# A hybrid two-block transformer on one core: every second chunk of the mixers' first products in halves, with its low half made by an accumulating transfer

## The reference

```python
h = rmsnorm(x, norm_mix[l])
(u_ssm, q_lat, kv_lat, k_rope, hg_q, hg_f, hg_i, hg_g, gate_logits) = jnp.split(h @ w_in[l], split_at, axis=-1)
y_ssm = s5_mixer(u_ssm, ...)
y_mla = mla_mixer(q_lat, kv_lat, k_rope, ...)
y_hg = hgrn2_mixer(hg_q, hg_f, hg_i, hg_g, ...)
gates = jax.nn.sigmoid(gate_logits)
x = x + (gates[0] * y_ssm + gates[1] * y_mla + gates[2] * y_hg) @ w_out[l]
x = x + memory_cross_attention(rmsnorm(x, norm_cross[l]), ...)
x = x + swiglu_ffn(rmsnorm(x, norm_ffn[l]), ...)
```

## Time and profile before

| | us |
|---|---|
| median of 3 runs | 1920.4 (1919.24 to 1921.8) |
| the profiled execution | 1917.89 |
| its span, first to last instruction | 1916.1 |
| PE busy | 1804.5 (94%) |
| DVE busy | 1232.3 (64%) |
| ACT busy | 867.0 (45%) |
| POOL busy | 277.2 (14%) |
| mean granted TensorE clock | 0.979 of full speed |

### The profile page before, as it was taken

The page is one execution under the profiler, slowest core; times in us unless marked ns, Lnnn a source line. Parts: engine busy times, 40 slices in busy tenths (PEclk is TensorE's granted clock), DMA queues, the critical chain, the costliest instruction groups (busy, mean ns, idle before and its releaser), DMA issues.

```text
span 1916.1 us, 27084 instructions
## 1 busy us (share of the span) xinstructions
PE 1804.5 (94%) x10038; PEld 1446.3 (75%) x10038; DVE 1232.3 (64%) x1895; ACT 867.0 (45%) x1413; POOL 277.2 (14%) x274
## 2 busy tenths in 40 slices
PE   7999989989999999999888999998899999989998
PEld 6676667569998866677577998656799864779987
DVE  7996755445667893855455566565677645566775
ACT  4224444355444422444355445336555543555553
POOL 4015453020000003557012000100100000010000
PEclk9999999999999999999999999998999999799999
DMA  6444442436566444445054666431455644135554
GB/s 160 130 130 152 133 152 89 143 105 180 160 187 188 119 127 142 133 133 177 28 191 116 194 184 192 147 110 56 141 177 163 193 153 121 56 107 170 169 187 138
DMA packets 192359, 274.61 MB, mean 143 GB/s; under 512 B 25616, under 2 KB 129540, under 8 KB 192228
## 3 DMA queue, kind: packets, MB, share of 16 engines
q1 hardware_dynamic: 191364, 269.86, 46.2%
q0 software_dynamic: 864, 3.02, 0.6%
HBM read 271.78 MB, written 1.05 MB: 142 GB/s over the span
## 4 chain that ended last, share of the span: by engine, by line
PE 80%; DVE 7%; ACT 6%; issue 3%; SPq 1%; POOL 1%; DMA 1%; DVEq 0%; ACTq 0%; POOLq 0%
PE bank L400 46%; PE bank L398 23%; DVE WL L1165 2%; ACT WH L1452 2%; PE bank L671 1%; PE bank L585 1%; PE bank L593 1%; PE bank L1021 1%; PE bank L871 1%; PE bank L1041 1%; PE bank L488 1%; ACT HTH L1452 1%; DVE bank L2117 1%; POOL WL L1165 0%; PE bank L654 0%
## 5 line engine op out<-in xcount | busy, mean ns | idle before, releaser
L1165 DVE TENSOR_TENSOR WL<-W,WH 128x1024 fp32r<-128x1024 f32 x304 | 372.5, 1225 | 241.9 <-ACT WH L1452 233.0
L1452 ACT ACTIVATE WH<-W 128x1024 fp32r<-128x1024 f32 x328 | 347.5, 1059 | 302.3 <-PE bank L400 267.2
L400 PE MATMUL bank<-HTH,WH 128*128 128x256 f32 x1536 | 437.6, 285 | 19.6 <-DVE WL L1165 9.5
L400 PE MATMUL bank<-HTL,WH 128*128 128x256 f32 x1536 | 434.5, 283 | 0.0
L400 PE MATMUL bank<-HTH,WL 128*128 128x256 f32 x1536 | 434.5, 283 | 0.0
L400 PEld LDWEIGHTS bank<-HTH,WH 128*128 128x128 f32 x1536 | 294.5, 192 | 25.2 <-DVE WL L1165 11.8
L400 PEld LDWEIGHTS bank<-HTL,WH 128*128 128x128 f32 x1536 | 294.7, 192 | 0.1
L400 PEld LDWEIGHTS bank<-HTH,WL 128*128 128x128 f32 x1536 | 294.6, 192 | 0.0
L400 PE MATMUL bank<-WH,HTL 128*128 128x512 f32 x672 | 261.4, 406 | 0.0
L400 PE MATMUL bank<-WH,HTH 128*128 128x512 f32 x480 | 192.7, 402 | 18.5 <-POOL WL L1165 5.7
L400 PE MATMUL bank<-WL,HTH 128*128 128x512 f32 x480 | 188.5, 393 | 0.0
(11 more groups left out here) (405 smaller groups left out, 2495.8 us busy)
## 6 DMA issues: line engine op xcount, KB each, us to landing
W<-in_w_in SPq DMA_DIRECT2D x132, 512.0 KB, 3.7
W<-in_ffn_w_gate_up SPq DMA_DIRECT2D x176, 256.0 KB, 3.4
W<-in_w_up SPq DMA_DIRECT2D x176, 256.0 KB, 3.6
W<-in_ffn_w_down SPq DMA_DIRECT2D x44, 512.0 KB, 3.7
W<-in_w_down SPq DMA_DIRECT2D x44, 512.0 KB, 4.2
W<-in_w_out SPq DMA_DIRECT2D x32, 512.0 KB, 3.4
W<-in_ssm_w_glu SPq DMA_DIRECT2D x16, 512.0 KB, 4.3
W<-in_x_w_kv SPq DMA_DIRECT2D x16, 512.0 KB, 3.4
```

Source lines behind the costliest of these rows:

```text
L400: m = pe.matmul(out, at_a(a[x]), at_b(b[y]), start=(start and i == 0), stop=(stop and i == 2), skip_group_check=True)
L1165: eng.tensor_tensor(WL[:, m % HSLOTS, 0:width], W[:, n % RSLOTS, 0:width], h, ALU.subtract)\
L1452: copy = lambda dst, src, scale=1.0: act.activation(dst, src, ACT.Copy, scale=scale)
```

## The change

Of each of the six groups hf, hq, hi, hg, kv and ql the second and the fourth chunk are now products in halves, with the split kind "dma". There are 12 such chunks in a layer. ACT copies the high part (`WH`), and then writes the negative of the high part into `WL`. POOL waits for that (`negative`) and issues a transfer that reads the same chunk of the weights from memory again and adds it to `WL`; its landing completes the low part. The chunk's buffer in `W` is free once ACT has copied the high part. POOL now makes `mix_half` earlier: after `mix_scaled` and after PE has finished u3. Then it issues the twelve transfers, in order, and only after them come, in layer 0, the inverse frequencies and rope angles, and in both layers `lat_rstd`. The core of the diff:

```diff
+            if who == "dma":
+                return f"low_dma{m % HSLOTS}", 16 * sum(1 for _, w in splits[m % HSLOTS:m + 1:HSLOTS] if w == "dma")
...
-                chunk_release[n] = (s, v)
+                chunk_release[n] = ("high", high_done(m)) if low == "dma" else (s, v)
...
+                    src, slot, how = act, lambda k: k, low
+                    if halves and k0 // kstep % 2:
+                        src, slot, how = halves, half_slot, "dma"
+                        if k0 == kstep:
+                            pe.wait_ge(sem["mix_halves"], l + 1)
+                    n, w = chunk(tag, rows(wname, l, k0, kstep, c0, cols), kstep, cols, how)
...
-                    token_out((name, l), "w_in", l, HTF, KT, c0, 512, low=None)
+                    token_out((name, l), "w_in", l, HTF, KT, c0, 512, low=None, halves=mix_half, how="dma")
...
+            def add_chunk(m):
+                n, _ = splits[m]
+                _, (src,), k, cols = chunks[n]
+                pool.wait_ge(sem["negative"], negative_done(m))
+                dst = WL[:, m % HSLOTS, 0:k * cols].rearrange("p (k n) -> p k n", k=k)
+                pool.dma_start(dst, src, accum_op=ALU.add).then_inc(sem[low_done(m)[0]], 16)
...
+                pool.wait_ge(sem["mix_scaled"], l + 1)
+                wait_full(pool, ("u", l, 3))
+                signal(halves_of(mix_half, HTF, 2, 6), "mix_halves", l + 1)
+                split_to(split_before["ql", l, 1])
+                if l == 0:
...
-                signal(halves_of(mix_half, HTF, 2, 6), "mix_halves", l + 1)
...
                     signal(copy(WH[:, m % HSLOTS, 0:width], W[:, n % RSLOTS, 0:width]), "high", high_done(m))
+                    if who == "dma":
+                        signal(copy(WL[:, m % HSLOTS, 0:width], WH[:, m % HSLOTS, 0:width].bitcast(F32), -1.0),
+                               "negative", negative_done(m))
```

More of the change, by code:

```diff
@@ L320, in low_done, with negative_done @@
         def low_done(m):
-            who = "dve" if splits[m][1] == "dve" else "pool"
-            return f"low_{who}", sum(1 for _, w in splits[:m + 1] if (w == "dve") == (who == "dve"))
+            who = splits[m][1]
+            if who == "dma":
+                return f"low_dma{m % HSLOTS}", 16 * sum(1 for _, w in splits[m % HSLOTS:m + 1:HSLOTS] if w == "dma")
+            if who == "dve":
+                return "low_dve", sum(1 for _, w in splits[:m + 1] if w == "dve")
+            return "low_pool", sum(1 for _, w in splits[:m + 1] if w in ("pool", "both"))
         def high_done(m):
             return sum(1 for _, w in splits[:m + 1] if w != "both")
+        def negative_done(m):
+            return sum(1 for _, w in splits[:m + 1] if w == "dma")
         @block.tensor
@@ L406, in token_out, with token_steps @@
                     pass
-            def token_steps(tag, wname, l, act, K, c0, cols, low="dve", kstep=2, halves=None):
+            def token_steps(tag, wname, l, act, K, c0, cols, low="dve", kstep=2, halves=None, how="both"):
                 ps = [begin(*tag, tt) for tt in range(TT)]
@@ L413, in token_steps @@
                     if halves and k0 // kstep % 2:
-                        n, w = chunk(tag, rows(wname, l, k0, kstep, c0, cols), kstep, cols, "both")
+                        n, w = chunk(tag, rows(wname, l, k0, kstep, c0, cols), kstep, cols, how)
                         src, slot = halves, half_slot
@@ L521, in feature_out, with feature_steps @@
                     pass
-            def feature_steps(tag, wname, l, act, K, c0, tiles, low="dve", kstep=2, extra=0):
+            def feature_steps(tag, wname, l, act, K, c0, tiles, low="dve", kstep=2, extra=0, halves=None):
                 cols = tiles * P + extra
@@ L529, in feature_steps @@
                 for k0 in range(0, K, kstep):
-                    n, w = chunk(tag, rows(wname, l, k0, kstep, c0, cols), kstep, cols, low)
+                    src, slot, how = act, lambda k: k, low
[3 more added lines that the diff above has]
+                            pe.wait_ge(sem["mix_halves"], l + 1)
+                    n, w = chunk(tag, rows(wname, l, k0, kstep, c0, cols), kstep, cols, how)
                     need_rows(act, k0 + kstep)
@@ L534, in feature_steps @@
                         for k in range(kstep):
-                            m = product(ps[j // 2][:, (j % 2) * S:(j % 2) * S + S], w, act,
-                                        lambda a: a[:, k, j * P:j * P + P], lambda b: b[:, k0 + k, :],
+                            m = product(ps[j // 2][:, (j % 2) * S:(j % 2) * S + S], w, src,
+                                        lambda a: a[:, k, j * P:j * P + P], lambda b: b[:, slot(k0 + k), :],
                                         k0 + k == 0 and j % 2 == 0, k0 + k == K - 1)
@@ L542, in feature_steps @@
                             for k in range(kstep):
-                                m = product(kr[:, tt * extra:(tt + 1) * extra], act, w,
-                                            lambda a: a[:, k0 + k, tt * P:tt * P + P],
+                                m = product(kr[:, tt * extra:(tt + 1) * extra], src, w,
+                                            lambda a: a[:, slot(k0 + k), tt * P:tt * P + P],
                                             lambda b: b[:, k, tiles * P:cols],
@@ L702, in mixer_in @@
                 def mixer_in(name, c0, tiles, extra=0):
-                    return feature_steps((name, l), "w_in", l, HTF, KT, c0, tiles, low=None, extra=extra)
+                    return feature_steps((name, l), "w_in", l, HTF, KT, c0, tiles, low=None, extra=extra,
+                                         halves=mix_half)
                 def mixer_tokens(name, c0):
-                    token_out((name, l), "w_in", l, HTF, KT, c0, 512, low=None)
+                    token_out((name, l), "w_in", l, HTF, KT, c0, 512, low=None, halves=mix_half, how="dma")
                 def ssm_u(*qs):
@@ L801, in _ @@
                     ssm_out(l, 3)
-                pe.wait_ge(sem["mix_halves"], l + 1)
                 for n in range(2):
@@ L1344, in split_to @@
                         both_parts(m)
+                        lows[0] = m + 1
+                    elif splits[m][1] == "dma":
+                        add_chunk(m)
                         lows[0] = m + 1
```

## The result

The changed kernel takes 1975.6 us (median of 4 runs, 1974.1 to 1978.0), the kernel before 1919.8 in the same comparison (1917.2 to 1921.8): a ratio of 1.030 [1.0285, 1.0314], **3.0% slower**. The profiled execution took 1975.23 us, span 1972.4, clock 0.966; before 1917.89, 1916.1 and 0.979. By these two it is 57.3 us slower, where I had forecast 36.5.

What follows compares the result with a forecast made beforehand. PE was taken to bound the kernel. Layer 0's +20.3 us and layer 1's +16.2 made +36.5 on the profiled 1917.9, 1954.4; with 2.5 for the median of runs, 1957 us, range 1933 to 1981.

Steps and rivals of the forecast that it cites:

- the first add: Layer 1, hf's second chunk: PE waits for POOL's input halves (5.0 us) and an add of 6.5 us; +8.0 us.
- the other adds: Later halved chunks: supply takes 14.1 us against PE's 12.6, but bank stalls give most back; +1.5 us a layer.
- the clock: Lower granted clock after PE's idleness at the head: +3 us in layer 1, +1 in layer 0.
- the forecast's test: Sign of error: the forecast is wrong if PE's idle time in the two stages does not grow by some 40 us.
- PE's savings: Halved chunks of the six groups take PE less time: 6.4 us a layer, 12.9 in both.
- ACT's wait ahead of rb: Head of each layer: ACT must await and copy hf's second chunk before evicting rb; +15.1 us layer 0, +4.75 layer 1.
- evictions behind the splits: ACT does both splits of the next group before evicting, so PE waits for banks; +9.1 us layer 0, +5.4 layer 1.
- DVE's state-space chain is shifted by the same 15 and so stays ahead: Layer 0 head: DVE's chain moves about 15 us later, as PE does, so PE does not wait for it.
- The extra 11 MB of reads find the transfer engines half idle: The adds' second reads of weights have room on the transfer engines; SP's order is not delayed by them.
- POOL in layer 0: Frequencies and angles, 22.1 us, moved behind the twelfth add, stay hidden ahead of the latent sums with 3 us to spare.
- Slow adds as a rival: Each add takes 9.6 us, lengthening a pair of chunks to 7.8 us from 6.3; time 1980 us, chance 0.16.

Runs made afterwards that it cites:

- e5: Changed kernel with ACT's evictions of rb and of each group moved ahead of the splits and no adding transfers issued (low half incomplete): 1914.5 us, ratio 0.9978.
- e2: Changed kernel, but ACT evicts rb, BT, the parameters and the first bu group before the first splits, except one split in layer 0: 1954.1 us, ratio 1.0203.
- e4: On top of e2, ACT evicts hf, hq, hi, hg and kv after the next group's first split, before its second: 1945.4 us, ratio 1.0156.
- e1: Changed kernel without the 24 adding transfers, PE waiting for ACT's negative instead; ACT's copies and order kept, output wrong: 1956.7 us, ratio 1.0205.
- the small add: e4 with each adding transfer cut from 512 KB to a 64 KB corner, still issued and waited for: 1923.7 us, ratio 1.0035.
- e6: Changed kernel's six groups in halves, but POOL makes both halves itself, with no adding transfer and no ACT split ahead of rb: 1969.9 us, ratio 1.026.

## Why the prediction came out as it did

The direction, the place and the kind of each wait were right, and 1975.6 is inside the range, near its upper end. The forecast was 19 us short. By the changed kernel's own trace, term by term (the clock as weighed above; some of PE's work hides in the ends of the waits):

| term, both layers | predicted, us | in the trace, us |
|---|---|---|
| the head, up to hf | +19.9 | +19.9 (14.3, 5.6) |
| PE's shorter matmuls | -12.9 | -11.0 |
| the first add, with POOL's halves | +8.0 | +9.2 |
| the other adds | +3.0 | +14.3 |
| banks | +14.5 | +8.7 |
| lower clock from hf to uq | +4 | +12.7 |
| lower clock at uq in layer 0 | 0 | +3.4 |
| sum | +36.5 | +57.2 |

Two terms were far too small, then, the other adds and the clock, and one was too large, the banks. Outside these stretches the two executions differ by amounts that no run ties to the change: by the clock, 3.9 us more lost in the rest of layer 0 and 9.3 less from layer 1's uq on, where PE also idles 3.8 us more. PE's idle time in the two stages grew by 50 us, for the "some 40" of the forecast's test.

The chain of experiments takes the loss apart in one order of undoing (another order would share the 16 us of mutual cover otherwise):

| step | predicted, us | measured, us |
|---|---|---|
| PE's savings, with what is late next | -12.9 | -4 (e5) |
| ACT's wait ahead of rb, both layers, and clock in layer 0 | +20.9 | +19 (e2) |
| evictions behind the splits | +14.5 | +9, not clear of noise (e4 against e2) |
| the adds, and clock in layer 1 | +14.0 | +34 (e5 against e4) |
| sum | +36.5 | +58 |

- **ACT's wait ahead of rb**: right, to the step. rb at 35.45 (36.1 forecast: the copies' end), the bu products at 47.23 (48.1), hf at 52.20 (53.0).
- **PE's savings**: the matmuls are as short as I had them. But "DVE's state-space chain is shifted by the same 15 and so stays ahead" was wrong: it was ahead by 0.4 us before, and PE saves 2.5 us ahead of the place. In the changed kernel itself PE, held up by an add, comes to the place at 82.43, 2.3 us after DVE. The kernels e1 and e5 show PE waiting there. In layer 1, 2.98 us go to POOL's halves, which I had put under the first add.
- **Evictions behind the splits**: the mechanism was right. In the changed kernel hi stands 6.3 us in layer 0 (4.5 forecast) and 1.08 in layer 1 (4.5), ql 0.26 in layer 0 (at 140.02, forecast 4.6) and kv 1.11 in layer 1 (0.9). Taking the evictions forward then saved clock rather than waiting, since the adds took over the wait.
- **The first add**: 9.24 us for 8.0. Landing was 6.0 us (4.6 to 7.9), for my 6.5; POOL's halves took 6.6 us beside DVE, for 5.0.
- **The other adds**: this is the step that failed. I had +1.5 us a layer; PE stood for them 7.8 us in layer 0 and 6.5 in layer 1, six waits of 2.0 to 2.8 us. The forecast's own supply of 14.1 us against PE's 12.6 already had the adds late in every pair; I then let the bank stalls pay for it, and they did not. That supply was about right or too short. The raw chunk issued at 62.6 landed after 8.4 us (4.9 forecast) and was copied by 73.2; its add, issued at 73.5, landed at 79.3, 16.7 us in all. For the chunk issued at 97.5 it was 14.2.
- **"The extra 11 MB of reads find the transfer engines half idle"** holds on average only. A full pair of chunks brings two raw ones: 44.3% of 1972.4 us for 269.86 MB on q1 is 3.24 us per MB, so 3.4 us a pair, and 3.3 for the add. Together 6.7, an estimate from the queues' shares, while PE works 6.2 to 6.3. But the engines were not full throughout. From 52 to 153 us, from hf to the end of ql, their shares are:
```profile
q0 software_dynamic: 3211, 5.72, 35.8%
q1 hardware_dynamic: 6515, 11.14, 34.7%
```
That is 0.7 in a stretch which the waits themselves have lengthened, with 0.9 to 1.1 where two raw chunks and an add are under way together. Whether PE's late adds come from the engines' rate or from the length of the way (raw chunk, two copies, issue, add) is not separated by these runs; the small add says only that the bytes make 23 of the 34 us. Raw chunks land later too (4.8 us for 3.7), but not for the adds alone: SP now issues them two at a time, and the pair of 97.06 and 97.47, with no add under way, took 3.7 and 4.6.
- **The clock**: +1 and +3 us were forecast, for the head. The trace has 7.6 and 5.2 from hf to uq, because most waits of 2 to 3 us are followed by a stretch at the lower clock as well, and the 6.29 us wait ahead of hi by a longer one.
- **POOL in layer 0**: forecast hidden with 3 us to spare. The frequencies and angles took 27.8 us (139.10 to 166.9) for 22.1, beside a busy DVE, and ended some 2 us after ACT had evicted the sums at 165.01, so the cover was gone. PE did not feel it: it has no wait from 154.91 until past 200, and the 3 us that uq's second part lost are clock.
- **Slow adds as a rival** (1980, chance 0.16) came nearest in time, by luck: it took 9.6 us per add, and the adds land in 6.0.

The Trainium skill's "DMA: Bandwidth & Descriptors" (Anatomy of one DMA) and "Collectives: The Full Stack" (The bandwidth ceiling) together gave an estimate of 4.4 us for an add to land; it took 6.0, and a plain copy of the same size took 4.2. The half rate that the Trainium skill's page on collectives gives for an add stands beside a measured 1.7 times the engines' time.

## What to carry to other kernels

A supplier with idle time on average can still be late in one stage. Add up, per step of that stage and not per kernel, its work (here engine time per pair of chunks, an estimated 6.7 us against PE's 6.3) and the length of the way from freeing a buffer to having the data (14 to 17 us against PE's 12.6). Price the clock behind each wait, and not only the wait. A look-ahead in an in-order engine is a wait for everything behind it; put the small instruction that releases others first, then the look-ahead (19 us here at the head). And before counting a saving on the fullest engine, read how far the second fullest is ahead of it at the next meeting point: here it was 0.4 us.

## What was not expected of the hardware

- A transfer that adds in float32 costs 1.7 times the engines' time of a plain one of the same bytes (26.6% against 15.7% of 140 us), lands in 6.0 us for 4.2, and keeps POOL busy 1.20 us at its issue for 0.71. The add of 64 KB still takes 3.1 us to land.
- Three 512 KB transfers issued within 1.2 us (two reads and an add) land in 3.8, 8.4 and 7.8 us.
- DVE's TENSOR_TENSOR of 128x1024 f32, 1.23 us alone, takes up to 3.28 us while POOL subtracts, and POOL's 2.4 become 3.2. Two copies on ACT and a transfer did the same work without slowing DVE: in the changed kernel the scans of the first state-space step took 0.69 us as before, in e6 1.87 and 1.34 on average (lines 2385 and 2386; 2.73 at most).
